# A two-block model on one core: seven slots for the experts' gate and up weights, four for down, loads queued as slots come free, one-hot columns built a round further ahead

## What is computed

```python
# block 1: 32 experts, 2 of them for each token; block 2: 64 experts, 8 for each token, plus one shared
hb = silu(xb @ w_gate[e]) * (xb @ w_up[e])      # 1024 -> 256, both
y  = (hb @ w_down[e]) * weight_of_token         # 256 -> 1024, added to its token's row
```

## Time and profile before

| | before |
|---|---|
| median of 3 runs | 1691.2 us (1686.55 to 1697.35) |
| the profiled execution | 1695.44 us, its span 1693.7 us |
| PE busy | 1298.3 us (77% of the span) |
| DVE busy | 534.1 us (32%) |
| ACT busy | 321.6 us (19%) |
| moved by DMA | 402.33 MB, 238 GB/s on average |
| mean granted TensorE clock | 0.868 of full speed |

### The profile page before, as it was taken

One profiled execution on the slowest core, in us unless ns is written; L12 is line 12 of the kernel. 1 busy time (PEld: TensorE's weight loads), 2 busy tenths in 40 slices (PEclk: granted clock), 3 DMA queues, 4 the chain that ended last, 5 costly groups with the idle time before them and its releaser, 6 DMA issues.

```text
span 1693.7 us, 24175 instructions
## 1 busy us (share of the span) xinstructions
PE 1298.3 (77%) x8269; PEld 681.4 (40%) x8269; DVE 534.1 (32%) x1536; ACT 321.6 (19%) x566; POOL 44.5 (3%) x90
## 2 busy tenths in 40 slices
PE   6998857477666574999389867988888888788654
PEld 4742233333323243854244435443444333334322
DVE  0004241422111104799543324222322222222222
ACT  2124432311001023110452213111111111111000
POOL 1001100200000000000000002000000000000000
PEclk9997768589878786999699977899999998989887
DMA  7457700496999494252003623647778876778993
GB/s 264 172 181 267 260 0 14 165 420 276 420 418 420 176 341 146 100 199 99 0 1 135 262 86 130 262 176 299 305 318 338 340 328 276 301 288 332 424 424 137
DMA packets 87952, 402.33 MB, mean 238 GB/s; under 512 B 10944, under 2 KB 19572, under 8 KB 59136
## 3 DMA queue, kind: packets, MB, share of 16 engines
q1 hardware_dynamic: 86608, 399.70, 59.7%
q10 hardware_dynamic: 816, 0.52, 0.1%
q0 software_dynamic: 384, 0.03, 0.0%
HBM read 399.15 MB, written 1.07 MB: 236 GB/s over the span
## 4 chain that ended last, share of the span: by engine, by line
PE 40%; DMA 12%; issue 3%; DVE 2%; SPq 2%; ACT 1%; DVEq 1%; PEldq 0%; ACTq 0%; PEld 0%
PE ps L1964 17%; PE ps L323 14%; DMA ring<-in_w_exp_gu 11%; PE ps L346 3%; PE ps L282 3%; PE ps L291 1%; PE ps L796 1%; DMA big<-mod 0%; SPq L687 0%; SPq L1543 0%; SPq L119 0%; SPq L102 0%; PE ps L272 0%; DMA posi<-in_positions 0%; ACT big L1660 0%
## 5 line engine op out<-in xcount | busy, mean ns | idle before, releaser
L323 PE MATMUL ps<-ring,big 128*32 128x512 f32 x2432 | 321.2, 679 | 173.6 <-DMA ring<-in_w_exp_gu 74.2
L323 PEld LDWEIGHTS ps<-ring,big 128*32 128x32 f32 x2432 | 91.7, 123 | 399.4 <-issue 397.2
L1964 PE MATMUL ps<-ring,big 128*128 128x512 f32 x464 | 202.0, 594 | 2.2 <-ACTq L776 1.1
L346 PE MATMUL ps<-big 128*32 128x512 f32 x1216 | 138.4, 595 | 0.0
L1964 PEld LDWEIGHTS ps<-ring,big 128*128 128x128 f32 x464 | 87.3, 190 | 110.4 <-issue 107.2
L282 PEld LDWEIGHTS ps<-big 128*128 128x128 bf16 x1920 | 116.7, 99 | 35.8 <-issue 21.0
L282 PE MATMUL ps<-big 128*128 128x128 bf16 x1920 | 126.8, 223 | 2.6 <-ACT big L190 1.5
L199 ACT ACTIVATE big<-ps 128x256 f32<-128x256 f32 x38 | 14.7, 386 | 526.8 <-PE ps L323 526.8
L1765 DVE SCALAR_TENSOR_TENSOR big<-big 128x256 f32<-128x256 f32 x240 | 105.6, 481 | 10.0 <-issue 1.3
L291 PE MATMUL ps<-parts,slot_tok 128*128 128x512 f32 x304 | 82.8, 416 | 21.4 <-DVEq L242 21.4
L190 ACT COPY big<-ps 128x512 f32<-128x512 f32 x80 | 47.0, 588 | 230.0 <-PE ps L282 230.0
(11 more groups left out here) (432 smaller groups left out, 1226.2 us busy)
## 6 DMA issues: line engine op xcount, KB each, us to landing
ring<-in_w_exp_gu SPq DMA_DIRECT2D x64, 2048.0 KB, 14.2
big<-in_w_exp_down SPq DMA_DIRECT2D x64, 1024.0 KB, 12.8
ring<-in_w_gate SPq DMA_DIRECT2D x32, 1024.0 KB, 12.4
ring<-in_w_up SPq DMA_DIRECT2D x32, 1024.0 KB, 14.9
big<-in_w_down SPq DMA_DIRECT2D x32, 1024.0 KB, 17.6
ring<-in_w_in SPq DMA_DIRECT2D x15, 2048.0 KB, 8.0
ring<-in_w_ada SPq DMA_DIRECT2D x12, 2048.0 KB, 7.9
ring<-in_w_in SPq DMA_DIRECT2D x7, 1536.0 KB, 13.9
```

What stands on the lines that cost most here:

```text
L323: last = pe.matmul(ps[rows, BG, :], m.xsT[:, k, rows], m.gu(m.gu_slot(at[j]), k), start=(k == 0), stop=(k == KC - 1), skip_group_check=True)
L346: last = pe.matmul(ps[rows, BD + n, :], m.hidT[:, k, rows], m.dring[:, at[j] % DOWN_SLOTS, k * D + n * 512:k * D + n * 512 + 512], start=( ...
L1964: last = pe.matmul(bank, lhs(k), rhs(k), start=(k == 0 and start), stop=(k == kk - 1))
```

## The change

Gate and up get seven slots: the six of the ring, and a seventh `gu7` in the memory that down slots 4 and 5 had. Down gets four. The total stays the same. Some of the second router's small tiles move to `gu7`'s place, where they are dead before it is loaded.

On SP each set now has two waits. When set i-1 is through gate and up, expert 4i+3's gate and up are loaded. When set i-1 is through down, all four down loads of set i are issued, and right behind them gate and up of 4i+4, 4i+5 and 4i+6, with no wait. The expert numbers of the first load behind each wait are read before it.

On DVE the one-hot columns are built two rounds ahead, in the middle of a round (after `S`, and after a wait for `T`, which says that PE has read the columns that they replace). `split` follows in the same round as `ys`.

```diff
-GU_SLOTS = DOWN_SLOTS = 6
+GU_SLOTS, DOWN_SLOTS = 7, 4
...
     def load_gu(at):
         slot, e = m.gu_slot(at), expert(at)
-        if at >= GU_SLOTS:
-            sp.wait_ge(ev(m.p + "gu"), window_end(sp, m, (at - GU_SLOTS) // PER))
-        elif m.before[slot]:
-            sp.wait_ge(ev(m.before[slot][0]), m.before[slot][1])
         m.load_gu(sp, slot, e, ev(f"w_in{slot}"))
...
-    for i in range(2, m.NQ):
-        for at in range(PER * i, PER * i + PER):
-            load_gu(at)
-        for at in range(PER * i, PER * i + PER):
-            load_down(at)
+    for i in range(1, m.NQ):
+        e = expert(PER * i + 3)
+        sp.wait_ge(ev(m.p + "gu"), window_end(sp, m, i - 1))
+        m.load_gu(sp, m.gu_slot(PER * i + 3), e, ev(f"w_in{m.gu_slot(PER * i + 3)}"))
+        done = window_end(sp, m, i - 1) * 2
+        e = expert(PER * i)
+        sp.wait_ge(ev(m.p + "down"), done)
+        sp.dma_start(m.dring[:, 0, :], m.w_down[bass.ds(e, 1)].rearrange("o (p k) n -> p (o k n)", p=P)).then_inc(
+            ev("w_in_d0"), 16)
+        for j in range(1, PER):
+            load_down(PER * i + j)
+        if i + 1 < m.NQ:
+            for j in range(PER, PER + 3):
+                load_gu(PER * i + j)
...
+    dve.tensor_copy(m.sc, m.scn)
+    dve.wait_ge(ev(m.p + "T"), 2)
+    onehot(1)
 
     def one(g):
 
-        if isinstance(g, int):
-            dve.wait_ge(ev(m.p + "T"), 2)
-        onehot(g + 1)
-        if not isinstance(g, int):
-            split(g)
-        dve.tensor_copy(m.sc, m.scn)
...
         dve.tensor_scalar(m.S, m.iota[:, T:2 * T], m.sc[:, 0:1], None, ALU.is_equal).then_inc(ev(m.p + "S"), 1)
+        dve.wait_ge(ev(m.p + "T"), g * 2 + 4)
+        onehot(g + 2)
         dve.wait_ge(ev(m.p + "down"), g * 2 + 2)
 
         dve.tensor_scalar(m.ys[:, 512:1024], ps[:, BD + 1, :], m.sc[:, 1:2], None, ALU.mult)
+        dve.drain()
+        dve.wait_ge(ev(m.p + "ya"), g + 1)
+        dve.tensor_copy(m.high, m.ys)
+        dve.tensor_copy(m.sc, m.scn)
+        dve.drain()
+        dve.tensor_tensor(m.low, m.ys, m.high.bitcast(F32), ALU.subtract)
+        dve.drain().then_inc(ev(m.p + "split"), 1)
     rounds(dve, m, one)
-    split(all_rounds(dve, m))
...
+            gu7 = take("gu7", [P, 4096])
+            m.gu_data = lambda slot: ring[:, slot, 0:4096] if slot < RING else gu7
```

More of the change, by code:

```diff
@@ L130, in load_down @@
         slot, e = at % DOWN_SLOTS, expert(at)
-        if at >= DOWN_SLOTS:
-            sp.wait_ge(ev(m.p + "down"), window_end(sp, m, (at - DOWN_SLOTS) // PER) * 2)
         sp.dma_start(m.dring[:, slot, :], m.w_down[bass.ds(e, 1)].rearrange("o (p k) n -> p (o k n)", p=P)).then_inc(
@@ L136, in moe_sp @@
     sp.wait_ge(ev(m.p + "order"), 1)
-    for at in range(PER, GU_SLOTS):
+    for at in range(PER, RING):
+        if m.before[m.gu_slot(at)]:
+            sp.wait_ge(ev(m.before[m.gu_slot(at)][0]), m.before[m.gu_slot(at)][1])
         load_gu(at)
@@ L140, in moe_sp @@
     sp.wait_ge(ev(m.p + "tok3"), 3 * TT)
-    for at in range(DOWN_SLOTS):
+    for at in range(PER):
         load_down(at)
-    for at in range(GU_SLOTS, 2 * PER):
-        load_gu(at)
-    for at in range(DOWN_SLOTS, 2 * PER):
-        load_down(at)
-    for i in range(2, m.NQ):
-        for at in range(PER * i, PER * i + PER):
-            load_gu(at)
-        for at in range(PER * i, PER * i + PER):
-            load_down(at)
+    load_gu(RING)
+    for i in range(1, m.NQ):
[12 more added lines that the diff above has]
+                load_gu(PER * i + j)
 def part_out(act, m, ev, part):
@@ L633, in load_gu1 @@
             for j, w in enumerate((A["w_gate"], A["w_up"])):
-                eng.dma_start(ring[:, slot, 2048 * j:2048 * j + 2048],
+                eng.dma_start(m1.gu_data(slot)[:, 2048 * j:2048 * j + 2048],
                               w[0][bass.ds(e, 1)].rearrange("o (p k) n -> p (o k n)", p=P)).then_inc(sem, 16)
         m1.load_gu, m1.gu_inc, m1.w_down = load_gu1, 32, A["w_down"][0]
-        m1.gu = lambda slot, k: ring[:, slot, 0:4096].rearrange("p (j k n) -> p j k n", j=2, k=KC)[:, :, k, :]
+        m1.gu = lambda slot, k: m1.gu_data(slot).rearrange("p (j k n) -> p j k n", j=2, k=KC)[:, :, k, :]
         mc = carver()
@@ L674, in build_program @@
         bc2 = m2.take("bc2", [P, 3, D])
-        rw2 = m2.take("rw2", [P, KC, 64])
-        rb2 = m2.take("rb2", [P, 64])
-        scr = m2.take("scr", [P, TT, 64])
-        cho = m2.take("cho", [P, TT, 64])
-        chm = m2.take("chm", [P, TT, 64])
-        g8 = m2.take("g8", [P, TT, 8, 8])
-        g1v = m2.take("g1v", [P, TT, 5, 8])
-        shs = m2.take("shs", [P, 2, T])
-        shT = m2.take("shT", [P, 2, T])
+        late = carver(DOWNS)
+        rw2 = late("rw2", [P, KC, 64])
+        rb2 = late("rb2", [P, 64])
+        scr = late("scr", [P, TT, 64])
+        cho = late("cho", [P, TT, 64])
+        chm = late("chm", [P, TT, 64])
+        g8 = late("g8", [P, TT, 8, 8])
+        g1v = late("g1v", [P, TT, 5, 8])
+        shs = late("shs", [P, 2, T])
+        shT = late("shT", [P, 2, T])
         out_tm = hn_tm
         def load_gu2(eng, slot, e, sem):
-            eng.dma_start(ring[:, slot, 0:KC * 512], A["w_exp_gu_2"][0][bass.ds(e, 1)].rearrange(
+            eng.dma_start(m2.gu_data(slot), A["w_exp_gu_2"][0][bass.ds(e, 1)].rearrange(
                 "o (p k) n -> p (o k n)", p=P)).then_inc(sem, 16)
         m2.load_gu, m2.gu_inc, m2.w_down = load_gu2, 16, A["w_exp_down_2"][0]
-        m2.gu = lambda slot, k: ring[:, slot, k * 512:(k + 1) * 512]
+        m2.gu = lambda slot, k: m2.gu_data(slot)[:, k * 512:(k + 1) * 512]
         def colblock(w, c0, n):
@@ L696, in build_program @@
         w_in = A["w_in"][0]
-        slot_total = [0] * RING
-        slot_user = [None] * RING
+        slot_total = [0] * (RING + 1)
+        slot_user = [None] * (RING + 1)
         n_loads = 0
@@ L721, in add_moe @@
             base = n_loads % RING
-            m.gu_slot = lambda at: (base + at) % GU_SLOTS
+            m.gu_slot = lambda at: (base + at % GU_SLOTS) % RING if at % GU_SLOTS < RING else RING
             for e in range(m.E):
```

7 lines of the change are left out of this document (removed).

## The result

| | before | after |
|---|---|---|
| median of 4 runs each, same chip | 1690.5 us (1686.6 to 1697.4) | 1653.6 us (1647.7 to 1655.4) |
| ratio | 1 | 0.9771 [0.9748, 0.9794] |
| profiled execution, its span | 1695.4, 1693.7 us | 1655.4, 1653.7 us |
| second MoE, first start to D of set 11 | 493.1 us | 462.6 us |
| clock, mean of the span | 0.868 | 0.875 |

The forecast was 1653. The 40 us between the two profiled spans lie in the second MoE's body by 30.5, in the first MoE (first to last set's start) by 3.0, in the stretch from there to the second MoE's start by 4.4, and 2 elsewhere. Of that 4.4, 2.3 us is a shorter wait at the first MoE's end; the rest is within what this stretch varies by (484 against 488 us from the first MoE's last down matmul on, in two profiles of one program, see `shift96`).

A forecast was written before the change was run, and what follows sets the result against it. DMA bounds the first MoE and the second's tail; PE's stops at new sets the second's body. Gains of 17.0, 11.5, 6.0, 4.0 and 0.7 less 1.0 make 38.2 us; off 1691.2 that gives 1653, range 1628 to 1678.

The forecast's parts named there:

- Part 1: Second MoE, PE's steps to new sets: one load behind gate-and-up instead of two shortens seven steps, 17.0 us.
- Rival A: PE needs some 4 us at every new set whatever the loads do: 1677 us, chance 0.15.
- Part 2: First rounds behind shortened steps: where PE stops 2 us or less its clock no longer falls, 11.5 us.
- Part 3: PE's waits for `split` and the one-hot go, as DVE builds the one-hot two rounds ahead: 6.0 us.
- Part 4: End of each MoE: `split` is out before DVE leaves its loops, 4.0 us for both ends.
- Part 5: Stretches bound by DMA: the first MoE gains 0.7 us, the second MoE's tail nothing.
- B: The clock falls after short stops too, so the clock's gain is 0: 1664 us, chance 0.15.
- C: Instruction packets shift or come sooner, and the 8.1 us steps fall as well: 1628 us, chance 0.07.
- D: Slower: down loads share the engines with three gate-and-up loads, land late and hold PE: 1785 us, chance 0.04.
- E: DVE becomes the bound and PE waits for it again at L291: 1663 us, chance 0.05.
- the signs: Second MoE's body: gate-and-up load waits fall from 35.1 to about 15 us, sets 33 to 35 apart, GB/s 340 to 380.

The follow-up runs named there:

- shift96: Changed kernel with 96 empty PE instructions ahead of the second MoE's sets, which leave nothing in the built program, so a repeat: 1656.8 us, ratio 0.9824.
- loop_to_n: Changed kernel with PE's loops of extra rounds run to their count instead of four passes: 1614.2 us, ratio 0.958.
- no_second_loop: Changed kernel without PE's second loop of extra rounds in all sets but the first of each MoE: 1604.9 us, ratio 0.9523.
- before_loop_n: Kernel before the change with PE's loops of extra rounds run to their count, loads and DVE as before: 1677.2 us, ratio 0.9928.
- dve_only: Kernel before the change, with its old loads and slots, given only the new DVE function: 1682.2 us, ratio 0.9966.

## Why the prediction came out, point by point

The total of 1653 for 1653.6 is in part luck: terms missed on both sides and made up for each other.

**Part 1, the steps: right in sum (16.3 for 17 less 1), wrong in how, and the sum is luck.** I took 0.9 us as the floor of the short steps, and had packets of instructions delay single sets. The runs show two floors. The landing is at 0.4 to 1.4 us behind D (`loop_to_n`, `no_second_loop`). Over it lies PE's own way to the next set (empty passes, counts, jump), 2.6 to 2.8 us, and 8.1 where the jump waits for code. The steps to sets 3, 4 and 11 therefore gained 1.7 us less each than predicted, that to set 2 1.0, that to set 5 0.7. What made it up was set 1, left at 5.0 in the prediction and now 1.0, and set 7, which fell to 2.8 and not to 4.5 (and set 6, to 2.6 and not 3). Two sentences failed there. "The packets should keep their places" did: the packet of the step to set 7 came at 1352.5, behind D, before, and comes in the half microsecond from 1321.5 now, 1.2 us ahead of D = 1322.7; L358, the jump, took 1.8 us there before, and 0.4 now. Set 1's moved in the same way. And "PE can start some 4 us behind the packet" did for the sets whose packet was in time: those to sets 3 and 4 come 3.7 and 4.2 us ahead of D, and PE still starts at D + 2.6, for the reason above. It held where PE stops in the jump. In the changed kernel the packet of set 8 came in the half microsecond from 1361.5, the jump ended at 1364.3 and PE began at 1365.4:

```profile
q8 instruction: 1, 0.02, 11.3%
```

There what the Trainium skill says ("Runtime: NRT & Kernel Launch", section "Instruction fetch mechanics") agrees: a jump to code that isn't loaded stops the engine, here in a jump of 5.9 us. Rival A was half right: "issue" did take the load's place at every set, with 2.6 us and not 4, and not for a fetch.

**Part 2, the clock: right in size (12.2 for 11.5), wrong in place, and half of it eaten.** In the five sets where I put 11.0 us, the clock gave 4.3: with steps of 2.6 where 0.9 was expected it still fell at some. Nor does it take the 3.4 us of idle time that I read from the earlier trace rows: over the 2.69 us of the step to set 12 a mean of 0.92 was granted, so it fell some 2.3 us into it. The rest came from sets 0 and 1 (3.5), 7 (2.8), 6 (1.5) and 8 to 10 (0.3), of which I had 0.5. Set 0's 1.7 is no gain of the change: its part is 8.8 us in the profile of `before_loop_n` and 7.07 in that of `dve_only`, which both have the old loads. What I hadn't thought of is that PE waits for code inside the parts, 6.6 us more than before: set 2's stayed at 12.6 and set 11's grew to 12.1. That left 5.6. The best proof of the mechanism is `loop_to_n`, where 7.07 us is the rule.

**Part 3, DVE: right.** Both waits are gone. `split` is out soon enough: the last copy of a `onehot` is done 2.5 us behind D, and the low half of `split` at D + 5.6, in the DVE timeline of the changed kernel around D = 1216.2:

```profile
1218.40 0.29 DVE L222 CAST big<-big 128x256 bf16<-128x256 f32 x1
1218.90 0.75 DVE L255 TENSOR_SCALAR big<-ps,big 128x512 f32<-128x512 f32 x1 [0.20 <-issue]
1219.73 0.69 DVE L258 CAST parts<-big 128x1024 fp32r<-128x1024 f32 x1
1220.34 0.16 DVE L259 COPY big<-big 128x2 f32<-128x2 f32 x1
1220.58 1.23 DVE L261 TENSOR_TENSOR parts<-big,parts 128x1024 fp32r<-128x1024 f32 x1
```

The prediction had D + 2.4 and D + 5.6. G to D lost 8.5 us where 6.0 were waits; the other 2.5 are some 0.2 in each of the twelve rounds that waited (9.4 to 9.0 us from G to D for a wait of 0.23): what a wait cost was a little more than its row says. With the ends of the MoEs 10 us were predicted; the half gave 6 alone and 9 to 17 on top of the loads, each no better known than half a per cent, some 8 us.

**Part 4, the ends: right, 3.7 for 4.0.** The last `combine` waits 6.8 us where it waited 8.2, and the one of the first MoE 5.6 for 7.9 (5 had been named as what would be left):

```profile
1641.72 3.44 PE L289 MATMUL ps<-parts,slot_tok 128*128 128x512 f32 x8 [6.77 <-issue]
```

**Part 5: the tail right, the first MoE too low.** D of set 11 to D of set 15 is 112.0 us for 112.2. In the first MoE I held D of set 1 fixed; its step fell from 7.7 to 5.8 and that to set 2 from 8.7 to 8.0, and the last set began 3.0 us nearer the first start, for 0.7 (the prediction names up to 4 us more for the case that set 1 starts earlier).

**Rivals and signs.** B's clock came true in part. Of C the packets did come sooner at the steps to sets 1 and 7; the 8.1 us steps did not fall, and that they could go altogether was only shown by other loops. D and E had no trace: no down load was waited for. Of the signs, waits for loads fell to nothing and not to 15 us, with 18.9 us of "issue" in their place at the same steps; GB/s rose less than named; and sets 3 to 7 start 34.7 to 36.9 us apart, not 33 to 35.

## What to carry to other kernels

A wait that one releaser ends hides the floors beneath it: before pricing its removal, ask for each what is next, and test by removing both (by the ratios the loop alone gives 12 us, the change alone 39, both 71). When the profile says "issue", read the engine's register and branch instructions by their source line: they told here what is work of the queue and what is a stop for code. Loops whose passes are mostly empty are not free: run them to their count. And since 128 instructions ahead moved `loop_to_n` by 1.3%, some 1% without their own cost, a gain under 1% should be seen at a second position before it is believed.

## What the runs showed of the hardware

- An empty pass of a loop over a body of some 330 instructions took PE's sequencer 0.75 us, reading a count 0.65 to 0.75, a jump over such a body 0.3 to 0.45 when the code was there. The sequencer was 2.7 us ahead of the matmuls at a set's end; three passes, two counts, the jump and the set's waits outlasted that by 2.6.
- Where the code wasn't there, the same jump took 5.8 to 6.0 us, at three neighbouring sets in the changed kernel. The place moves with the code, 32 instructions a set, and comes back after eight sets. With loops run to their count and nearly the same packets (110 for 111) the jump took 3.9 us at most, and up to 6.2 with the old loads.
- A 2 MiB load, first in an idle queue, took 8.6 us from issue to landing, so one queued at G, 9.0 us ahead of D, is about in time, and one queued at D holds PE for 9.
- Of the five stops of 2.6 to 2.8 us to sets 3 to 7 in the changed kernel the clock fell behind one (set 5). In `loop_to_n` it was the same with two of 3.55 us: 7.07 behind that to set 6, 8.77 behind that to set 7. A stop of 1.9 us, 1.05 us of work and a second stop, in set 2, also brought it down, in the second stop:

```profile
1142.90:1145.20 2.30, 0.00 (x2) 0.00 (x1) 2.14 (x4) 0.00 (x0) 0.00 (x0) 0.50 0.97 385
```
